# Gate and up projections of a feed-forward layer by seven block products in place of eight, in two passes over the tokens

## Chip, cores and metric

One Trainium2 chip, one core of it. The metric is the device time of one execution in microseconds (us), median over runs. The granted clock of TensorE is given as a share of full speed.

## What is computed

One step of a one-layer encoder over 1024 prompt tokens and 32 sample tokens (1056 in all, width 1024): input projection, two kinds of attention, output projection with residual, and a feed-forward part. The change lies in the last:

```python
def residual_tail(h, oa, ob, g_out_a, g_out_b, w_out, g_ffn, w_gate, w_up, w_down):
    mixed = jnp.concatenate([rmsnorm(oa, g_out_a), rmsnorm(ob, g_out_b)], axis=-1)
    h = h + mixed @ w_out
    u = rmsnorm(h, g_ffn)
    return h + (jax.nn.silu(u @ w_gate) * (u @ w_up)) @ w_down
# then rmsnorm(h, g_final); everything float32; w_gate, w_up: 1024 x 2816, w_down: 2816 x 1024
```

## The kernel before

A matrix product in float32 is made of three TensorE products of type fp32r: each operand x is split into a rounded half `hi` (made on ACT by a copy that rounds) and the rest `lo` = x - `hi` (made on DVE), and `product` (L603 to L606) adds hi·hi, hi·lo and lo·hi in one PSUM bank. In `product`'s lines L604 is the first, L605 the second, L606 the third. PSUM has eight banks of 512 float32 columns.

Five programs run side by side, one for each engine (`@block.tensor` for PE, `scalar` for ACT, `vector` for DVE, `gpsimd` for POOL, `sync` for SP, which issues the loads and stores), each strictly in the order written, tied by semaphores (`wait_ge`, `then_inc`).

The stage before the feed-forward part (`out_product`, `turn_mixed`, `turn_residual`) makes h by tiles of 128 tokens. `turn_residual` (L984) turns each tile twice on PE, by eight 128x128 transposes each: h itself (L987 to L990, into banks 4 and 5, kept as the columns to which the result is added, `outs`) and the normalised u (banks 6 and 7), which ACT and DVE split into `f_hi` and `f_lo`.

The feed-forward part takes the 2816 hidden columns in eleven pairs of 128-column blocks (`FFQ`), tokens along the free dimension in three chunks of 384, 384 and 288 (`CHUNKS`). For each pair q, `gate_up(q)` (L1009) makes gate and up of both blocks: four weights of 1024x128 by eight k-blocks by three chunks. Silu is ACT's (L1459), the product gate·up DVE's (L1877), and h is split by ACT (L1465) and DVE (L1880). Then `down(q - 1)` (L1030) multiplies the hidden pair before with the down weights, 24 groups (eight output blocks by three chunks) of six matmuls, in banks 6 and 7 by turns, and DVE adds each group to `outs` (`add_one`, L1883). Each weight is loaded once (`ffn_load`, L2324, three raw buffers of 512 KB), and split by ACT (L1092) and DVE (L1522, 128x1024). POOL has nothing to do in this part. The last pair's groups use four banks, 4 to 7 (`last_down`), and between them and behind them `turn_out` turns the result back to rows, which ACT squares and DVE scales (`last_out`).

## Time and profile before

| | |
|---|---|
| runs | 1424.62, 1425.41, 1426.76 us (median 1425.41) |
| profiled execution: span | 1425.3 us |
| PE busy | 1389.4 us (97%), 9041 matmuls |
| DVE, ACT, POOL busy | 572.3, 484.7, 213.8 us |
| stage before the feed-forward part | 567 to 635 us of the span |
| feed-forward part | from 635.1 us to the end |
| moved by DMA | 97.64 MB, mean 69 GB/s |

The profile comes from one execution; the page gives no other time of it than the span, from its first to its last instruction. Busy times are shares of an engine's own time. A matmul's duration in it covers its whole way through the array, and the next one starts long before it ends, so the rate is read from starts.

### The profile page before, as it was taken

What the parts mean: (1) busy time and instruction counts of PE and PEld (TensorE: products, weight loads), DVE (VectorE), ACT (ScalarE), POOL (GpSimd) and SP (SyncE); (2) the same over time, 40 slices, a digit from 0 to 9 for tenths busy, and PEclk for the clock granted to TensorE, in tenths of its full rate; (3) what the DMA queues carried; (4) which work ended last, traced back from release to release, by engine and by line L of the source; (5) the groups of instructions that cost most, each with busy time, mean ns of one, the idle gap of its engine ahead of it and who ended that gap; (6) DMA issues with size and microseconds to landing.
All of it is one profiled execution on the core that took longest, in us unless ns stands there. A gap on an engine that the chain in (4) does not pass through costs nothing.

```text
span 1425.3 us, 22561 instructions
## 1 busy us (share of the span) xinstructions
PE 1389.4 (97%) x9041; PEld 1288.1 (90%) x9041; DVE 572.3 (40%) x1340; ACT 484.7 (34%) x1049; POOL 213.8 (15%) x318
## 2 busy tenths in 40 slices
PE   7999999999999899999999999999999999999998
PEld 5988898788878677889999999999999999999997
DVE  6345634242323433562333434342424252525156
ACT  6356555655554552563212121212121212121103
POOL 3145551644443230000000000000000000000000
PEclk9999999999999899999999999999999999999999
DMA  7621124212120444314202020202020202020003
GB/s 202 115 67 38 32 78 156 81 43 80 51 83 15 150 163 135 109 46 132 61 30 68 22 74 16 74 16 74 16 74 16 75 16 74 16 74 15 30 1 122
DMA packets 110255, 97.64 MB, mean 69 GB/s; under 512 B 15936, under 2 KB 96928, under 8 KB 109640
## 3 DMA queue, kind: packets, MB, share of 16 engines
q1 hardware_dynamic: 110152, 96.20, 23.0%
q8 instruction: 72, 1.18, 0.4%
q14 instruction: 31, 0.25, 0.1%
HBM read 77.07 MB, written 19.21 MB: 68 GB/s over the span
## 4 chain that ended last, share of the span: by engine, by line
PE 91%; DVE 3%; DMA 2%; ACT 2%; issue 2%; POOL 1%; SPq 0%; ACTq 0%; DVEq 0%
PE ps L604 28%; PE ps L605 26%; PE ps L606 26%; PE ps L808 2%; DMA cb<-c_scratch 1%; PE ps L738 1%; PE ps L956 1%; PE ps L820 1%; PE ps L685 1%; PE ps L897 1%; PE ps L776 1%; DVE ps L1650 1%; DMA ob<-o_scratch 1%; ACT sp_x L1279 0%; PE ps L703 0%
## 5 line engine op out<-in xcount | busy, mean ns | idle before, releaser
L1891 DVE TENSOR_TENSOR outs<-outs,ps 128x384 f32<-128x384 f32 (+1 forms) x264 | 134.5, 509 | 108.3 <-PE ps L606 108.0
L1877 DVE TENSOR_TENSOR gu<-ps,sg 128x384 f32<-128x384 f32 (+1 forms) x66 | 34.6, 524 | 237.8 <-PE ps L606 237.8
L2055 POOL TENSOR_TENSOR pl_x<-sp_x,ph_x 128x512 fp32r<-128x512 f32 (+5 forms) x120 | 102.3, 866 | 170.4 <-ACT sp_x L1279 169.0
L1465 ACT ACTIVATE h_hi<-gu 128x384 fp32r<-128x384 f32 (+1 forms) x66 | 32.9, 498 | 222.4 <-DVE gu L1877 222.4
L1278 ACT ACTIVATE ph_x<-ps,negc 128x512 fp32r<-128x512 f32 (+5 forms) x120 | 63.0, 525 | 84.5 <-PE ps L820 84.5
L1459 ACT ACTIVATE sg<-ps 128x384 f32<-128x384 f32 (+1 forms) x66 | 30.5, 465 | 171.7 <-PE ps L606 171.7
L604 PE MATMUL ps<-f_hi,ff0hi 128*128 128x384 f32 (+1 forms) x264 | 85.7, 325 | 0.0
L604 PE MATMUL ps<-f_hi,ff2hi 128*128 128x384 f32 (+1 forms) x264 | 85.6, 324 | 0.0
L604 PE MATMUL ps<-f_hi,ff3hi 128*128 128x384 f32 (+1 forms) x264 | 85.6, 324 | 0.0
L604 PE MATMUL ps<-f_hi,ff1hi 128*128 128x384 f32 (+1 forms) x264 | 85.6, 324 | 0.0
L605 PE MATMUL ps<-f_lo,ff0hi 128*128 128x384 f32 (+1 forms) x264 | 85.3, 323 | 0.0
L605 PE MATMUL ps<-f_lo,ff1hi 128*128 128x384 f32 (+1 forms) x264 | 85.2, 323 | 0.0
L605 PE MATMUL ps<-f_lo,ff2hi 128*128 128x384 f32 (+1 forms) x264 | 85.2, 323 | 0.0
L605 PE MATMUL ps<-f_lo,ff3hi 128*128 128x384 f32 (+1 forms) x264 | 85.2, 323 | 0.0
L606 PE MATMUL ps<-f_hi,ff0lo 128*128 128x384 f32 (+1 forms) x264 | 85.2, 323 | 0.0
L606 PE MATMUL ps<-f_hi,ff1lo 128*128 128x384 f32 (+1 forms) x264 | 85.1, 322 | 0.0
L606 PE MATMUL ps<-f_hi,ff2lo 128*128 128x384 f32 (+1 forms) x264 | 85.1, 322 | 0.0
L606 PE MATMUL ps<-f_hi,ff3lo 128*128 128x384 f32 (+1 forms) x264 | 85.1, 322 | 0.0
L604 PE MATMUL ps<-h_hi,ff4hi 128*128 128x384 f32 (+1 forms) x240 | 82.2, 342 | 0.6 <-DVE outs L1894 0.5
L604 PE MATMUL ps<-h_hi,ff5hi 128*128 128x384 f32 (+1 forms) x240 | 78.2, 326 | 0.0
L1092 ACT ACTIVATE ff4hi<-raw 128x1024 fp32r<-128x1024 f32 x10 | 10.6, 1060 | 197.0 <-PE ps L606 197.0
L605 PE MATMUL ps<-h_lo,ff5hi 128*128 128x384 f32 (+1 forms) x240 | 77.5, 323 | 0.0
(303 smaller groups left out, 3837.5 us busy)
## 6 DMA issues: line engine op xcount, KB each, us to landing
raw<-in_w_gate SPq DMA_DIRECT2D x22, 512.0 KB, 4.5
raw<-in_w_up SPq DMA_DIRECT2D x22, 512.0 KB, 5.0
raw<-in_w_down SPq DMA_DIRECT2D x22, 512.0 KB, 3.9
raw<-in_w_in SPq DMA_DIRECT2D x14, 512.0 KB, 4.0
cb<-c_scratch SPq DMA_DIRECT2D x4, 1312.0 KB, 7.1
xt<-in_x_prompt SPq DMA_DIRECT2D x8, 512.0 KB, 4.7
out<-outb SPq DMA_DIRECT2D x16, 256.0 KB, 2.8
ob<-o_scratch SPq DMA_DIRECT2D x16, 256.0 KB, 3.1
```

Source lines behind the costliest of these rows:

```text
L604: pe.matmul(out, wh, xh, start=start, stop=False)
L605: pe.matmul(out, wh, xl, start=False, stop=False)
L606: return pe.matmul(out, wl, xh, start=False, stop=stop)
L685: mm = pe.transpose(ps[0:m, b, (2 * kv + x) * P:(2 * kv + x + 1) * P], ot_w[kv][:, x * m:(x + 1) * m], ident[:])
L738: pe.matmul(ps[0:rows, 2 + kv, 0:2 * m].rearrange("p (x q) -> p x q", x=2), keys[hs, k0:k0 + rows], queries[half][hs, :, q], start=(part = ...
L808: pe.matmul(ps[0:rows, b + h, 0:n], keys[i % 2][hs, k0:k0 + rows], queries[i % 2][hs, q], start=(part == 0), stop=False)
L1278: act.activation(ph_x[2 * (v % 2) + h][0:rows, 0:n], ps[0:rows, b + h, 0:n], ACT.Exp, bias=decay, scale=-1.0)
L1459: act.activation(sg[c][:, 0:n], bank(c, n), ACT.Silu).then_inc(S["g_sg"], 1)
L1465: act.activation(h_hi[par][:, f, c0:c0 + n], gu[(f + c) % 2][:, 0:n], ACT.Copy).then_inc(S["g_hi"], 1)
L1877: dve.tensor_tensor(gu[(f + c) % 2][:, 0:n], bank(3 + c, n), sg[c][:, 0:n], ALU.mult)\
L1891: add = dve.tensor_tensor(y, y, bank(b, whole * P).rearrange("p (t m) -> p t m", t=whole), ALU.add)
L2055: pool.tensor_tensor(pl_x[at][0:rows, 0:n], sp_x[at][0:rows, 0:n], ph_x[at][0:rows, 0:n].bitcast(F32), ALU.subtract).then_inc(S["x_pl"], 1)
```

## The change

Gate and up of one 128-column block are the two block rows of a 2x2 matrix A: row 1 is gate, row 2 is up, column 1 the upper 512 rows of the weights, column 2 the lower. The input u (1024 x tokens) is cut in the same way: k halves by token halves. The 2x2 product of blocks is then made by seven products and 15 additions instead of eight products. The changed kernel

- runs over the tokens in two passes, 512 tokens in halves of 256 and 544 in halves of 272 (`HALF_OF`), with 22 sets in each (`SETS` = 44, one set for each block of 128 hidden columns), so all gate, up and down weights are loaded and split twice;
- makes per set seven products (`ffn_product`), each of four k-blocks and one token half, in banks 0 to 5 by turns; ACT copies two of the seven banks out (`copy_out`), DVE adds the other five (`add_bank`), POOL adds two more parts (`add_fourth`), then silu and gating are done in SBUF (`silu`, `gated`);
- makes four sums of weight blocks per set on POOL (`weight_sums`, from raw weights in `fraw`, 1 MB in two buffers), and four sums of input blocks per pass (`input_sum`); ACT and DVE split seven weight blocks of 128x512 per set into eleven slots (`SLOTS`), and seven input blocks per pass;
- makes down groups (`down_group`) in the midst of the products, one output half (four output blocks) of a hidden pair per set: four groups of 512 columns in pass 0, eight of 272 in pass 1, always in banks 6 and 7; the down weights' `lo` halves are made by POOL (`down_lo`, 128x1024) from the single buffer `draw`;
- no longer turns h on PE: h goes to DRAM (`x2_dram`) by rows, comes back at the end (`hrow`), and the turned result is added to it by rows (`add_row`); rows 0 to 3 are turned in set 24, added there and scaled in set 25.

The core of the diff:

```diff
-            def turn_residual(t):
-                pe.wait_ge(S["c_h2"], 2 * (t + 1))
-                if t >= 1:
-                    pe.wait_ge(S["d_y"], 4 * t)
-                rows_to_columns(t, xc[t % 2], (4, 5), S["c_t2"])
...
+            def ffn_product(g, i):
+                p = pass_of(g)
+                n, e = HALF_OF[p], 7 * g + i
+                pe.wait_ge(S["fw_lo"], e + 1)
+                if g % NF == 0:
+                    pe.wait_ge(S["u_lo"], 7 * p + U_ORDER.index(i) + 1)
+                if e >= SPARE:
+                    pe.wait_ge(*bank_read(*divmod(e - SPARE, 7)))
...
+                w, (uh, ul) = fw[e % SLOTS], fu[i]
+                for k in range(4):
+                    mm = product(bank(e % SPARE, n), w[:, 0, k, :], w[:, 1, k, :], uh[:, k, 0:n], ul[:, k, 0:n],
+                                 k == 0, k == 3)
+                mm.then_inc(S["f_pe"], 1)
...
+            def down_group(n, q, j):
...
+                pe.wait_ge(S["f_hl"], 4 * pg + 4)
+                pe.wait_ge(S["dw_lo"], n - 1)
+                if at >= 2:
+                    pe.wait_ge(S["y_add"], at - 1)
...
+            for g in range(SETS):
+                for i in range(7):
+                    ffn_product(g, i)
...
+                    elif g >= 2 and 2 <= i < 6:
+                        down_piece(g, i - 2)
...
+            def weight_sums(g):
...
+                pool.wait_ge(S[f"fw_in{g % 2}"], 32 * (g // 2 + 1))
+                if g >= 1:
+                    pool.wait_ge(S["fw_lo"], 7 * (g - 1) + 5)
+                pool.tensor_tensor(s1, a21, a22, ALU.add).then_inc(S["fw_sum"], 1)
+                pool.wait_ge(S["fw_sum"], 4 * g + 1)
+                pool.tensor_tensor(s2, s1, a11, ALU.subtract).then_inc(S["fw_sum"], 1)
+                pool.tensor_tensor(s3, a11, a21, ALU.subtract).then_inc(S["fw_sum"], 1)
+                pool.wait_ge(S["fw_sum"], 4 * g + 2)
+                if g >= 1:
+                    pool.wait_ge(S["fw_lo"], 7 * (g - 1) + 6)
+                pool.tensor_tensor(s4, a12, s2, ALU.subtract).then_inc(S["fw_sum"], 1)
...
+            def add_fourth(g):
+                n, par = HALF_OF[pass_of(g)], g % 2
+                for x in range(2):
+                    pool.wait_ge(S["f_x"], 2 * g + 2)
+                    pool.wait_ge(S["f_add"], 5 * g + 3 + x)
+                    part = x23[par][:, x, 0:n]
+                    pool.tensor_tensor(part, part, p7[:, 0:n], ALU.add).then_inc(S["f_p7"], 1)
+            def down_lo(n):
...
+                pool.wait_ge(S["dw_hi"], n - 1)
+                pool.tensor_tensor(dw[n % 2][:, 1, :, :], draw[:], dw[n % 2][:, 0, :, :].bitcast(F32), ALU.subtract)\
+                   .then_inc(S["dw_lo"], 1)
...
+            for g in range(SETS):
...
+                if g + 2 < SETS:
+                    weight_sums(g + 2)
+                add_fourth(g)
+                down_lo(g + 1)
...
+            def load_ffn_raw(g):
...
+                elif g >= 2:
+                    sp_.wait_ge(S["fw_lo"], 7 * (g - 2) + 7)
+                    sp_.wait_ge(S["fw_sum"], 4 * (g - 2) + 4)
+                for mat, src in enumerate((w_gate_v, w_up_v)):
+                    sp_.dma_start(fraw[g % 2][:, mat, :, :], src[:, :, f * P:(f + 1) * P]).then_inc(S[f"fw_in{g % 2}"], 16)
+            def load_down_raw(n):
...
+                if n > 2:
+                    sp_.wait_ge(S["dw_lo"], n - 2)
...
+            for k in range(SETS):
+                load_ffn_raw(k + 2)
+                if k >= 1:
+                    load_down_raw(k + 2)
```

**Order on SP.** The loads of two steps of the feed-forward part, before:

```order
L2106 DMA raw_61<-in_w_down 128x1024 [waits cw_lo]
L2106 DMA raw_62<-in_w_down 128x1024 [waits cw_lo]
L2106 DMA raw_60<-in_w_gate 128x8x128 [waits cw_lo]
L2106 DMA raw_61<-in_w_up 128x8x128 [waits cw_lo]
L2106 DMA raw_62<-in_w_gate 128x8x128 [waits cw_lo]
L2106 DMA raw_60<-in_w_up 128x8x128 [waits cw_lo]
```

and now, two sets in pass 0 (`fraw` the raw gate and up weights, `draw` the raw down weights):

```order
L2635 DMA draw<-in_w_down 128x2x512 [waits dw_lo]
L2626 DMA fraw_175<-in_w_gate 128x8x128 [waits fw_sum,fw_lo]
L2626 DMA fraw_175<-in_w_up 128x8x128
L2635 DMA draw<-in_w_down 128x2x512 [waits dw_lo]
L2626 DMA fraw_176<-in_w_gate 128x8x128 [waits fw_sum,fw_lo]
L2626 DMA fraw_176<-in_w_up 128x8x128
```

Before, every load waited for the split of the same kind of weight (`cw_lo`, counted on DVE); now each pair of gate and up loads stands behind a down load that waits for POOL's `down_lo` (`dw_lo`).

**Order on POOL.** POOL had no row in the feed-forward part; its last ones were the attention's. Now one set in pass 0 has (`sums` the weight sums, `x` and `p` the parts that `add_fourth` adds, `dw` the split down weights):

```order
L2330 TENSOR_TENSOR sums<-fraw_176 128x512 [waits fw_lo,fw_in0]
L2332 TENSOR_TENSOR sums<-sums,fraw_176 128x512 [waits fw_sum]
L2333 TENSOR_TENSOR sums<-fraw_176 128x512
L2337 TENSOR_TENSOR sums<-fraw_176,sums 128x512 [waits fw_lo,fw_sum]
L2363 TENSOR_TENSOR x_0_190<-x_0_190,p_179 128x256 [waits f_add,f_x] x2
L2370 TENSOR_TENSOR dw_218<-draw,dw_218 128x1024 [waits dw_hi]
```

Four sums, two adds and one down half repeat in every set, all from SBUF to SBUF.

**Order on DVE.** Before, between two pairs (`ff` the split weights, `gu` the product of gate and up):

```order
L1522 TENSOR_TENSOR ff0lo<-raw_60,ff0hi 128x1024 [waits cw_hi]
L1522 TENSOR_TENSOR ff1lo<-raw_61,ff1hi 128x1024 [waits cw_hi]
L1522 TENSOR_TENSOR ff2lo<-raw_62,ff2hi 128x1024 [waits cw_hi]
L1877 TENSOR_TENSOR gu_191<-ps,sg_187 128x384 [waits g_lo,g_sg,g_mm]
L1880 TENSOR_TENSOR h_lo_186<-gu_191,h_hi_185 128x384 [waits g_hi]
L1877 TENSOR_TENSOR gu_190<-ps,sg_188 128x384 [waits g_lo,g_sg,g_mm]
L1880 TENSOR_TENSOR h_lo_186<-gu_190,h_hi_185 128x384 [waits g_hi]
L1877 TENSOR_TENSOR gu_191<-ps,sg_189 128x288 [waits g_lo,g_sg,g_mm]
L1880 TENSOR_TENSOR h_lo_186<-gu_191,h_hi_185 128x288 [waits g_hi]
```

and now, from the last weight half of a set in pass 0 to the second bank add of the next (`fw` the split weights, `sg` the gate part, `x` the up part, `y` the result):

```order
L2007 TENSOR_TENSOR fw_192<-sums,fw_192 128x512 [waits fw_hi]
L2043 TENSOR_TENSOR sg_220<-sg_220,x_0_190 128x256 [waits f_p7,f_sg]
L2065 TENSOR_TENSOR y<-y,ps 128x512 [waits y_add,d_pe]
L2050 TENSOR_TENSOR h_lo_215<-sg_220,h_hi_214 128x256 [waits f_hh]
L2033 TENSOR_TENSOR x_0_190<-x_0_190,ps 128x256 [waits f_p7,f_pe]
L2043 TENSOR_TENSOR sg_220<-sg_220,x_0_190 128x256 [waits f_add,f_sg]
L2007 TENSOR_TENSOR fw_193<-sums,fw_193 128x512 [waits fw_hi]
L2007 TENSOR_TENSOR fw_194<-sums,fw_194 128x512 [waits fw_hi]
L2050 TENSOR_TENSOR h_lo_215<-sg_220,h_hi_214 128x256 [waits f_hh]
L2033 TENSOR_TENSOR sg_216<-x_199,ps 128x256 [waits f_x,f_pe]
L2007 TENSOR_TENSOR fw_195<-sums,fw_195 128x512 [waits fw_hi]
L2033 TENSOR_TENSOR x_1_222<-x_199,ps 128x256 [waits f_x,f_pe]
```

The gating now reads only SBUF and waits for POOL (`f_p7`), and the add to `y`, the hidden half and the bank adds of the next products stand behind it.

## Rows read from the trace of the kernel before

**Rows 1.** The page: busy time by engine (share of span), and the clock granted to PE in 40 slices.

```profile
span 1425.3 us, 22561 instructions
PE 1389.4 (97%) x9041; PEld 1288.1 (90%) x9041; DVE 572.3 (40%) x1340; ACT 484.7 (34%) x1049; POOL 213.8 (15%) x318
...
PEclk9999999999999899999999999999999999999999
```

**Rows 2.** Busy times of each engine, granted clock, DMA share and GB/s, in three stretches.

```profile
567.00:635.10 68.10, 67.78 (x376) 55.74 (x376) 41.80 (x72) 37.97 (x86) 0.00 (x0) 1.00 0.27 83
...
705.00:775.00 70.00, 70.00 (x433) 69.59 (x432) 26.05 (x50) 11.59 (x18) 0.00 (x0) 1.00 0.16 46
...
1370.00:1388.00 18.00, 16.66 (x103) 15.70 (x102) 11.09 (x27) 0.00 (x0) 0.00 (x0) 1.00 0.00 1
```

**Rows 3.** Timeline of PE in one gate and up weight: start us, us, form.

```profile
999.74 0.34 PE L604 MATMUL ps<-f_hi,ff3hi 128*128 128x384 f32 x1
...
1007.11 0.29 PE L604 MATMUL ps<-f_hi,ff3hi 128*128 128x288 f32 x1
...
1010.30 0.34 PE L604 MATMUL ps<-h_hi,ff4hi 128*128 128x384 f32 x1
```

**Rows 4.** Timeline of PE: six matmuls of 256 columns in a row.

```profile
100.10 0.28 PE L604 MATMUL ps<-ph_w,vs_hi 128*128 128x256 f32 x1
...
100.69 0.28 PE L606 MATMUL ps<-ph_w,vs_lo 128*128 128x256 f32 x1
```

**Rows 5.** Timeline of PE: matmuls of 512 columns, then turned tiles (x8).

```profile
621.95 0.40 PE L604 MATMUL ps<-wo_hi,m_hi 128*128 128x512 f32 x1
...
626.15 1.03 PE L956 MATMUL ps<-ident,xb 128*128 128x128 f32 x8
627.02 1.04 PE L956 MATMUL ps<-ident,raw 128*128 128x128 f32 x8
```

**Rows 6.** Groups by form, DVE: xcount, busy us, mean ns, idle before.

```profile
L1583 DVE TENSOR_TENSOR vw_lo<-cache_v,vw_hi 128x256 fp32r<-128x256 f32 x4 | 1.7, 423 | 3.0 <-ACT vw_hi L1225 3.0
L1585 DVE TENSOR_TENSOR vw_lo<-outb,vw_hi 128x512 fp32r<-128x512 f32 x8 | 5.6, 702 | 13.8 <-ACT vw_hi L1225 13.8
```

**Rows 7.** Groups by form, ACT and POOL.

```profile
L1360 ACT ACTIVATE ob<-ob 128x512 f32<-128x512 f32 x8 | 5.0, 626 | 4.5 <-DMA ob<-o_scratch 4.5
...
L1247 ACT ACTIVATE ph_w<-sp_w 128x256 fp32r<-128x256 f32 x60 | 24.6, 409 | 29.0 <-DVE sp_w L1662 29.0
...
L2055 POOL TENSOR_TENSOR pl_x<-sp_x,ph_x 128x512 fp32r<-128x512 f32 x48 | 60.8, 1287 | 61.2 <-ACT sp_x L1279 61.2
L2004 POOL TENSOR_TENSOR pl_w<-sp_w,ph_w 128x256 fp32r<-128x256 f32 x60 | 43.0, 738 | 41.4 <-ACT sp_w L1248 41.3
...
L1989 POOL TENSOR_TENSOR cw1lo<-raw,cw1hi 128x1024 fp32r<-128x1024 f32 x9 | 21.8, 2425 | 40.1 <-ACT cw1hi L1092 39.8 <-issue 0.2
```

**Rows 8.** Timelines of POOL and of DVE: two-SBUF-input DVE instructions beside POOL.

```profile
17.80 2.41 POOL L1989 TENSOR_TENSOR cw0lo<-raw,cw0hi 128x1024 fp32r<-128x1024 f32 x1 [9.47 <-ACT cw0hi L1092]
29.68 2.41 POOL L1989 TENSOR_TENSOR cw1lo<-raw,cw1hi 128x1024 fp32r<-128x1024 f32 x1 [9.47 <-ACT cw1hi L1092]
...
17.23 1.28 DVE L1528 TENSOR_TENSOR u_lo<-ps,u_hi 128x512 fp32r<-128x512 f32 x2
...
19.31 1.98 DVE L1734 SCALAR_TENSOR_TENSOR xn<-xt,small,gains 128x1024 f32<-128x1024 f32 x1
...
31.20 1.98 DVE L1734 SCALAR_TENSOR_TENSOR xn<-xt,small,gains 128x1024 f32<-128x1024 f32 x1
```

**Rows 9.** SP's queue: three loads issued in a row, and their landing (DMA view, 649 to 659).

```profile
650.05 0.37 SPq L2106 DMA_DIRECT2D raw<-in_w_gate  x1
...
651.09 1.32 SPq L2106 DMA_DIRECT2D raw<-in_w_gate  x1
...
raw<-in_w_gate SPq DMA_DIRECT2D x2, 512.0 KB, 5.4
```

**Rows 10.** The stretch 460 to 480: PE's busy time and clock (columns as in Rows 2).

```profile
460.00:480.00 20.00, 14.70 (x107) 10.85 (x108) 11.00 (x25) 13.39 (x27) 5.16 (x6) 0.74 0.46 147
```

811 lines of the change are left out of this document (511 added, 300 removed).

## The prediction, made before the change was run

> **What bounds the kernel now.** I read the page first: PE is busy for 97% of the span at an almost undisturbed clock, DVE for 40%, and POOL's 213.8 us all lie before the feed-forward part [rows 1, 2]. Then the windows: in a step of two blocks (705 to 775) PE has no idle time, DVE works 26 us, ACT 12 us, POOL nothing [rows 2]. So the feed-forward part lasts as long as its matmuls stream, and what counts is start to start, not the duration of one (they overlap).
>
> Start to start: 42 matmuls of 384 columns in 7.37 us are 0.1755 us each, 24 of 288 columns in 3.19 us are 0.1329 [rows 3]; 256 columns take 0.118 (five intervals in 0.59) [rows 4]; 512 take 0.2333 (18 intervals in 4.20) [rows 5]. For 272 I take 0.1255, between 256 and 288.
>
> Check on before: gate and up are 2112 matmuls of 384 and 1056 of 288, 511.0 us; down 1056 and 528, 255.5 us; together 766.5.
>
> **The change on PE.** Seven products of four row blocks replace eight: per set 84 matmuls, so 22 x 84 of 256 (218.1 us) and 22 x 84 of 272 (231.9), together 450.0 against 511.0: **-61 us**. Down keeps its columns: 528 of 512 and 1056 of 272, 255.7, no change. A set with down then needs 15.5 us in pass 0 (84 x 0.118 + 24 x 0.2333) and 16.6 in pass 1 (132 x 0.1255). The residual's eight turns per tile go; eight take 0.87 us [rows 5], nine tiles at most 7.3. That stage is PE's (67.8 busy of 68.1) but ACT has 38 us there [rows 2] and now gets seven input splits: I count **-6**, between 0 and -7.3. Near 1370 to 1388 PE stands 1.3 us [rows 2], tied to the old last weights: -1. The turned output tiles stay. If nothing else waits: 1425 - 68 = **1357**.
>
> The Trainium skill (TensorE: Matmul & The Clock Gate, Back-to-back issue gap) gives N/2.4 + 2.5 ns from matmul to matmul. By that estimate gate and up would fall from 473 to 416 us, a gain of 57; the rows are about 8% slower than it, and the sum goes by the rows.
>
> **The change beside PE, and why cover may end.** In sets 2 to 43 each engine's order repeats. Per set DVE has seven weight halves of 128x512, four adds of results (eight narrower ones in pass 1), five bank adds, two gatings and two hidden halves. An instruction of 512 columns takes 0.70 us, one of 256 takes 0.42 [rows 6]; behind another it adds 0.60 (1.28 for two, less 0.68 for one [rows 8]) and 0.34 (the same 0.08 less). That is 6.6 + 3.1 = 9.7 us. ACT: 0.63 and 0.41 each [rows 7], seven weights, one 1024 wide, six narrow ones, about 8 us. POOL, new here: four sums of 1.27, two adds of 0.74, one down half of 2.42 [rows 7], 9.0 us. Each alone fits into 15.5, hidden by PE's matmuls. Three things chain them.
>
> (1) *A ring through SP's queue.* The load of the down weights waits until POOL has made the last down half (single buffer), and SP's gate and up loads for the set after next stand behind it in the queue; POOL's next sums need these. Three loads issued in a row at 650.05 have landed at 651.09 + 5.4 = 656.5 [rows 9], 6.4 us; with two semaphore hops 6.6. Ring: 6.6 + 5.1 + 1.5 + 2.4 + 0.3 for waits on POOL's own results = **15.9 us**, against PE's 15.5: +0.4 in pass 0, nothing in pass 1.
>
> (2) *DVE and POOL hold each other up.* At 19.31 a DVE instruction with both inputs in SBUF takes 1.98 us: POOL's instruction began at 17.80 and ended at 20.21, and DVE ended 1.08 later. The same at 31.20 (POOL 29.68 to 32.09), 1.98 again, while DVE's pair at 17.23, one input in PSUM, kept its 1.28 beside POOL [rows 8]. So such a DVE instruction waits out POOL's, and ends some 0.2 earlier than its duration behind it. The weight halves (`weight_lo_ffn`), gatings (`gated`) and hidden halves (`hidden_lo`), 11 of DVE's 20 instructions and 6.6 us if each stood alone, are of this kind; before, POOL was idle here. No row shows POOL held by DVE. I take it to work both ways, since DVE was held to the very end of POOL's instruction, as by something that one of them has to itself; one way alone is a bound below. The Trainium skill (SBUF — State Buffer, Who interferes with whom) has a rule against this change: the two engines take turns at a shared pair of ports, and whoever comes second waits for the whole instruction of the first. By that rule, the trace agrees for DVE (1.98 against 1.28).
>
> (3) *The gating sits behind POOL's adds.* DVE's `gated(g, 1)` waits for POOL's second add of `add_fourth(g)`, after which POOL starts `down_lo` at once and holds DVE for another 2.2 us; queued behind it on DVE are the y add that frees a down bank, the hidden half and the bank adds, for which PE and ACT wait.
>
> By hand, from the end E of a down half: DVE's held weight half 0.5, gating, y add, hidden half, bank add, gating: +2.5; ACT's hidden, bank copy and two weights 2.0: +4.5; two weight halves (the first overlaps) and the hidden half: +5.6, where the first down group of an even set may start; bank add, ACT's silu and weight: +6.9. The loads land at +6.6 and POOL's sums begin. From here sums and weight halves alternate: sum to 7.9, half 8.4, sum 9.6, bank add, y add and half 10.1, sum 11.3, half 11.8, sum 13.0, bank add and half 13.5, POOL's first add 14.1, y and bank adds 14.5, second add 15.2, down half: **E' = 17.6**. Without the lock it is 15.9. So in pass 0 a set takes 17.6 instead of 15.5: 20 sets, **+42** (with one direction 16.6: +22; unlocked +8). In pass 1 the narrow adds lengthen it to about 18.0 against 16.6; 20 sets, **+29** (bounds 0 and +45).
>
> Smaller terms: the first sets run from loads issued within set 0, so set 2's first down group waits about 5 us for sums, hidden and down halves: **+5** (0 to 10). Where the passes meet, four POOL sums of 2.4 and seven DVE halves of 1.2 (128x1024, twice the 512 form) come into the ring: **+12** (5 to 20). Rows 0 to 3 are added and scaled in sets 24 and 25, eight DVE instructions of about 1.2, half of them of the locked kind: **+5**. The last 16 groups alternate between two banks where 24 had four, then rows are squared, rooted and scaled: **+3** (-3 to 8). DMA moves twice the gate and up weights, about 1.5 MB a set; the share before is 0.16 [rows 2], so bandwidth costs nothing, only the latency above does.
>
> Sum: 1357 + 42 + 29 + 5 + 12 + 5 + 3 = **1453 us**. It is made against the profiled span, 1425.3, which is the median of the runs shown (1425.41) within 0.1.
>
> **Rivals.**
> *Faster: the lock falls beside the ring.* If DVE mostly meets POOL while it waits for loads, or POOL's instructions are not held, DVE keeps up and the ring of 15.9 is all: 1357 + 8 + 0 + 4 + 10 + 3 + 3 = **1385**. For it: DVE has 5.8 of 15.5 us free, and POOL stands 6.6 us of each ring. Against: DVE has just its serial stretch (E to +6.9) in that pause, and its weight halves come with the sums. It decides for a set time under 16.8 us on the mean of both passes, where the added waits no longer eat the 68.
>
> *Slower still: PE's clock.* In my forecast PE stands about 4 us ahead of the first down group of every second set. At 460 to 480, with 5.3 us idle in the stretch, the clock was 0.74 instead of 1.00 [rows 10]. A fall to the lower level in each of these gaps costs PE some 2 us in a pair of sets, which delays the bank add that POOL waits for: 20 pairs, +40, **1493**. Against: most gaps would be split between several waits. The Trainium skill (TensorE: Matmul & The Clock Gate, Why this matters for your kernels) also warns of idle gaps between bursts of matmuls.
>
> *The seven products save nothing on PE* would need matmuls of 256 columns no faster than 0.135 us; [rows 4] speaks against it, and I give it no chance of its own.
>
> **How the numbers follow.** Forecast 0.50, the lock beside the ring 0.38, the clock 0.12. Forecast's own range: 1422 (one direction only in both passes, small terms low) to 1480. The other cases extend the range to 1380 and 1495; below lies some of the first rival, above some of the last. About 0.2% (2.9 us) is what a measurement of this kernel can tell from no change: 0.04 lies there, the lower edge of the forecast gives 0.01 to faster, so 0.39 faster, 0.57 slower.
>
> **What would show it.** Right: PE's 256-column matmuls 0.118 apart; in pass 0 idle PE ahead of a down group in even sets, ended by DVE's hidden half; set times near 17.6 and 18.0; DVE's weight halves at 0.7 alone and up to 2 us beside POOL; POOL idle some 6.6 us a set until gate and up weights land; SP waiting for POOL's down half. Wrong: PE without gaps in pass 0, or set times at 15.5 to 16 (then the rival); a granted clock clearly below 1 in the feed-forward part (then the other); or gaps that end with an engine I have not named.

## The result, and the profile after

The changed kernel takes **1566.9 us** (median of 4 runs, 1564.4 to 1572.1), the kernel before 1426.1 beside it: ratio 1.0996, 95% interval [1.0971, 1.102]. It is slower by 10%. The prediction said slower, with 1453 in a range up to 1495: the direction held, the size did not, and the time lies 72 us above the range. The profiled run took 1564.7, its span is 1562.9.

Short names below: a *set* is one block of 128 hidden columns, its time read from the first matmul of product 0 to the next such; a *weight half* is the `hi` (ACT) or `lo` (DVE) part of a 128x512 weight, the *down half* is `down_lo`, the *hidden half* `h_hi` or `h_lo`; *gating* is `gated`, a *bank add* `add_bank`, a *y add* `add_group`. In the changed kernel `product`'s three lines are L702 to L704; line numbers in a view are those of the kernel that it shows, so they shift a little from run to run.

The page of the changed kernel, where [rows 1] stood:

```profile
span 1562.9 us, 26068 instructions
PE 1380.0 (88%) x9497; PEld 1245.5 (80%) x9497; DVE 945.2 (60%) x1760; ACT 674.2 (43%) x1462; POOL 685.3 (44%) x634
...
PEclk9999999999999999989999999987998999999998
```

PE is busy for 1380 us where it was 1389, although gate and up should cost it 61 us less: much of the difference went by at a lower clock. The windows, in four stretches of the feed-forward part (sets 0 to 3, 4 to 19, 20 to 27, and from set 43 to the end); columns as in [rows 2]:

```profile
632.13:708.12 75.99, 58.63 (x395) 54.60 (x394) 57.14 (x77) 34.08 (x69) 42.67 (x30) 0.87 0.28 78
...
708.12:1009.10 300.98, 266.36 (x1731) 244.65 (x1730) 224.53 (x320) 111.64 (x224) 165.03 (x113) 0.93 0.31 85
1009.10:1210.46 201.36, 154.71 (x994) 146.17 (x993) 142.30 (x192) 70.75 (x131) 94.07 (x62) 0.86 0.28 84
...
1506.64:1562.90 56.26, 36.61 (x270) 35.56 (x268) 33.87 (x55) 13.34 (x26) 7.17 (x5) 0.87 0.17 61
```

The first number behind start and end is the length of the stretch. Sets 4 to 19 take 301.0 / 16 = 18.8 us each, where PE needs 15.5. Sets 28 to 42 take 19.75 each (1210.46 to 1506.64), where PE needs 16.6. The eight sets around the pass change take 201.

The matmuls themselves did what [rows 4] said. PE's timeline: from the first to the last of these there are eight intervals of 256 columns in 0.94 us, 0.1175 each.

```profile
817.27 0.28 PE L702 MATMUL ps<-fu5hi,fw 128*128 128x256 f32 x1
...
818.21 0.28 PE L704 MATMUL ps<-fu5hi,fw 128*128 128x256 f32 x1
```

The view of waits (engine, line, releaser: us in total, times, longest):

```profile
POOL sums L2330 <- DMA fraw<-in_w_up: 294.9, 34, 26.4
...
DVE fw L2007 <- ACT fw L1543: 181.3, 171, 5.0
...
PE ps L702 <- DVE h_lo L2050: 91.2, 21, 10.1
...
POOL sums L2330 <- DVE fw L2007: 71.2, 9, 10.6
...
PE ps L702 <- DVE y L2065: 30.6, 18, 4.4
```

PE stands for DVE's hidden half, as forecast, 21 times. POOL's first sum of a set waits mostly for the load, as forecast too. The second row is the one that I had not counted: DVE waits about one microsecond, 171 times, for ACT's half of a weight. At 804.16 below this is the time that ACT takes behind DVE's last bank add for a silu and the half; DVE's own half starts 0.65 us after the start of ACT's.

The instruction groups show the lock (us in all, mean ns of one); the same forms alone take 700 and 420 ns [rows 6], 2420 ns on POOL [rows 7]:

```profile
L2007 DVE TENSOR_TENSOR fw<-sums,fw 128x512 fp32r<-128x512 f32 x176 | 195.0, 1129 | 138.4 <-ACT fw L1543 138.4
...
L2007 DVE TENSOR_TENSOR fw<-fraw,fw 128x512 fp32r<-128x512 f32 x132 | 153.5, 1175 | 42.9 <-ACT fw L1543 42.8
...
L2043 DVE TENSOR_TENSOR sg<-sg,x 128x256 f32<-128x256 f32 (+1 forms) x88 | 68.7, 781 | 8.4 <-POOL x L2363 3.5 <-DVE x L2033 0.5
```

One turn of POOL, in its timeline (start us, us, engine, line, operation; in brackets how long the engine stood before it, and what ended that); beside it DVE's instructions of the same time, then ACT's:

```profile
803.30 0.74 POOL L2363 TENSOR_TENSOR x<-x,p 128x256 f32<-128x256 f32 x1 [1.31 <-DVE sg L2033]
803.99 2.43 POOL L2370 TENSOR_TENSOR dw<-draw,dw 128x1024 fp32r<-128x1024 f32 x1
814.65 1.32 POOL L2330 TENSOR_TENSOR sums<-fraw 128x512 f32<-128x512 f32 x1 [8.22 <-DMA fraw<-in_w_up]
816.04 1.64 POOL L2332 TENSOR_TENSOR sums<-sums,fraw 128x512 f32<-128x512 f32 x1
817.63 1.76 POOL L2333 TENSOR_TENSOR sums<-fraw 128x512 f32<-128x512 f32 x1
819.36 1.75 POOL L2337 TENSOR_TENSOR sums<-fraw,sums 128x512 f32<-128x512 f32 x1
821.08 1.43 POOL L2363 TENSOR_TENSOR x<-x,p 128x256 f32<-128x256 f32 x2
822.46 2.89 POOL L2370 TENSOR_TENSOR dw<-draw,dw 128x1024 fp32r<-128x1024 f32 x1
```

```profile
804.16 2.81 DVE L2007 TENSOR_TENSOR fw<-sums,fw 128x512 fp32r<-128x512 f32 x1 [1.01 <-ACT fw L1543]
806.89 0.41 DVE L2043 TENSOR_TENSOR sg<-sg,x 128x256 f32<-128x256 f32 x1
...
809.02 0.43 DVE L2043 TENSOR_TENSOR sg<-sg,x 128x256 f32<-128x256 f32 x1 [0.46 <-DVE x L2033]
810.73 1.29 DVE L2007 TENSOR_TENSOR fw<-sums,fw 128x512 fp32r<-128x512 f32 x2 [1.28 <-ACT fw L1543]
```

```profile
809.48 0.42 ACT L1592 ACTIVATE h_hi<-sg 128x256 fp32r<-128x256 f32 x1 [1.73 <-DVE sg L2043]
809.81 0.37 ACT L1577 ACTIVATE x<-ps 128x256 f32<-128x256 f32 x1
810.07 1.14 ACT L1543 ACTIVATE fw<-sums 128x512 fp32r<-128x512 f32 x2
```

From the end of one down half (806.42) to that of the next (825.35) are 18.9 us. POOL waits 8.2 for the load, the four sums take 6.4 instead of 5.1 (so DVE holds POOL too: 1.75 against 1.29 alone in [rows 7]), the adds 1.4, the down half 2.9. In all of sets 4 to 19 POOL's turn goes through the load: on the mean 7.6 us of landing, 6.2 of sums, 2.4 of adds with their waits, 2.6 of down half, together 18.8. In every second set the adds take 3.1 to 3.5 us, because one of them waits for DVE's bank add (803.30), and that for PE. On DVE the weight half at 804.16 is held to 806.97, 2.8 us instead of 0.7, with the gating behind it. And ACT stands 1.7 us for DVE's second gating before it comes to two weight halves that depend on no gating at all; DVE then waits 1.3 for these.

PE in the same pair, and its clock (windows; the number before the last two is the granted clock):

```profile
830.38 0.50 PE L702 MATMUL ps<-h_hi,dw 128*128 128x512 f32 x1 [4.16 <-DVE h_lo L2050]
```

```profile
826.20:830.40 4.20, 0.04 (x2) 0.02 (x1) 2.82 (x8) 1.72 (x4) 0.00 (x0) 1.00 0.97 268
830.40:832.40 2.00, 2.00 (x6) 1.62 (x7) 0.99 (x3) 1.46 (x3) 0.00 (x0) 0.64 0.94 225
832.40:834.40 2.00, 2.00 (x11) 1.91 (x10) 1.79 (x3) 0.00 (x0) 1.43 (x2) 0.51 0.03 8
834.40:838.40 4.00, 4.00 (x27) 3.61 (x27) 2.11 (x4) 2.34 (x4) 4.00 (x3) 1.00 0.00 0
```

Behind 4.2 us of standing PE runs 4 us at a mean of 0.575 (the lower level, 1.2 GHz, for most of it) and loses 4 x 0.425 = 1.7 us. So, by this estimate, the gap costs PE 5.9 us, not 4.2.

### The profile page after: what moved, and what is told of

It reads as the page before. It is cut to its first block, busy times and chain, and to the rows that moved or that the text cites. A ratio compares the mean times of both kernels' runs of the same rounds, so it can differ in the third digit from the quotient of the medians.

```text
span 1562.9 us, 26068 instructions
## 1 busy us (share of the span) xinstructions
PE 1380.0 (88%) x9497; PEld 1245.5 (80%) x9497; DVE 945.2 (60%) x1760; ACT 674.2 (43%) x1462; POOL 685.3 (44%) x634
## 4 chain that ended last, share of the span: by engine, by line
PE 51%; DVE 19%; issue 11%; ACT 6%; DMA 4%; POOL 2%; SPq 1%; DVEq 0%; ACTq 0%; POOLq 0%
PE ps L702 15%; PE ps L703 14%; PE ps L704 14%; DVE fw L2007 5%; ACT fw L1543 3%; DVE sg L2043 3%; PE ps L906 2%; DVE y L2065 2%; DMA fraw<-in_w_up 2%; DVE h_lo L2050 2%; DVE x L2033 2%; DVE sg L2033 1%; PE ps L836 1%; DMA cb<-c_scratch 1%; ACT x L1577 1%
## 5 line engine op out<-in xcount | busy, mean ns | idle before, releaser
L702 PE MATMUL ps<-h_hi,dw 128*128 128x272 f32 (+1 forms) x528 | 186.6, 353 | 125.8 <-DVE h_lo L2050 91.2
L2007 DVE TENSOR_TENSOR fw<-sums,fw 128x512 fp32r<-128x512 f32 x176 | 195.0, 1129 | 138.4 <-ACT fw L1543 138.4
L702 PEld LDWEIGHTS ps<-h_hi,dw 128*128 128x128 f32 x528 | 106.8, 202 | 140.0 <-DVE h_lo L2050 95.6
L704 PE MATMUL ps<-h_hi,dw 128*128 128x272 f32 (+1 forms) x528 | 181.6, 344 | 0.0
L703 PE MATMUL ps<-h_lo,dw 128*128 128x272 f32 (+1 forms) x528 | 181.0, 343 | 0.0
L2007 DVE TENSOR_TENSOR fw<-fraw,fw 128x512 fp32r<-128x512 f32 x132 | 153.5, 1175 | 42.9 <-ACT fw L1543 42.8
L1543 ACT ACTIVATE fw<-fraw 128x512 fp32r<-128x512 f32 x132 | 82.2, 626 | 122.3 <-PE ps L704 102.1
L2065 DVE TENSOR_TENSOR y<-y,ps 128x272 f32<-128x272 f32 (+1 forms) x240 | 117.7, 511 | 18.6 <-PE ps L704 18.6
L704 PEld LDWEIGHTS ps<-h_hi,dw 128*128 128x128 f32 x528 | 107.7, 204 | 8.8
L2370 POOL TENSOR_TENSOR dw<-draw,dw 128x1024 fp32r<-128x1024 f32 x44 | 111.2, 2528 | 5.1 <-ACT dw L1568 5.1
L703 PEld LDWEIGHTS ps<-h_lo,dw 128*128 128x128 f32 x528 | 107.6, 204 | 4.4
L1543 ACT ACTIVATE fw<-sums 128x512 fp32r<-128x512 f32 x176 | 104.4, 619 | 1.1 <-PE ps L704 0.9
L702 PE MATMUL ps<-u_hi,cw1hi 128*128 128x384 f32 (+1 forms) x216 | 75.1, 348 | 1.0 <-POOL cw1lo L2222 1.0
L702 PE MATMUL ps<-u_hi,cw0hi 128*128 128x384 f32 (+1 forms) x216 | 75.0, 347 | 0.0
```

Of the source, the lines that this page charges most:

```text
L702: pe.matmul(out, wh, xh, start=start, stop=False)
L703: pe.matmul(out, wh, xl, start=False, stop=False)
L704: return pe.matmul(out, wl, xh, start=False, stop=stop)
L1543: act.activation(fw[e % SLOTS][:, 0, :, :], weight_block(g, i), ACT.Copy).then_inc(S["fw_hi"], 1)
L2007: dve.tensor_tensor(lo, weight_block(g, i), hi.bitcast(F32), ALU.subtract).then_inc(S["fw_lo"], 1)
L2065: dve.tensor_tensor(dst, dst, bank(6 + at % 2, width), ALU.add).then_inc(S["y_add"], 1)
```

## The experiments

All start from the changed kernel. The times are medians, the ratios (with 95% interval) against the kernel before, run beside them.

**1. The queue.** In SP's loop:

```diff
+            load_ffn_raw(2)
             for k in range(SETS):
-                load_ffn_raw(k + 2)
+                load_ffn_raw(k + 3)
                 if k >= 1:
                     load_down_raw(k + 2)
```

> Only the order on SP's queue changes: gate and up weights of a set are loaded ahead of the down weights that wait for POOL's down half, so that the ring through the queue is open. Theory 1 (ring of load, sums, adds and down half, stretched by the lock between DVE and POOL): POOL stands no longer 6.6 to 8 us a set for the landing; the held work that DVE and POOL must take in turn is 6.6 + 9.0 = 15.6 us a set, so a set falls from 18.8 to 16 to 17 in pass 0 and from 19.75 to 17 to 18 in pass 1: about -45 and -40, and some 10 at the start and where the passes meet, 1460 to 1490. Rival (the serial chain of DVE, ACT and POOL behind product 5 sets the set's time, the loads only fill a pause that is there anyway): POOL's pause stays and ends with DVE in place of the DMA, under 20 us are gained, 1550 or more.

1567.0 us, 1.0993 [1.0967, 1.102]: not a microsecond. POOL's 295 us of waiting for the load shrank to the one wait at the start, and the time stands in other rows:

```profile
POOL sums L2330 <- DVE fw L2007: 244.9, 42, 10.6
...
POOL x L2363 <- DVE x L2033: 118.7, 42, 12.8
...
POOL sums L2330 <- DMA fraw<-in_w_up: 26.2, 1, 26.2
```

So the rival held: another path of the same length lies beside the ring through the queue, and my own theory of one ring falls here. One turn of it in POOL's timeline:

```profile
813.12 1.37 POOL L2330 TENSOR_TENSOR sums<-fraw 128x512 f32<-128x512 f32 x1 [5.74 <-DVE fw L2007]
...
820.92 1.07 POOL L2363 TENSOR_TENSOR x<-x,p 128x256 f32<-128x256 f32 x1 [1.62 <-DVE x L2033]
```

The sums' buffer is single, and POOL may write it only when DVE has made the weight halves from it; that ends its first wait. But with the sums done POOL stands again, in every set, for a bank add of DVE, which waits for PE's product. So the path does not close through the buffer of the sums. It goes from POOL's down half to DVE's held weight half and gating, ACT, DVE's weight halves and hidden half, PE, DVE's bank add and POOL's adds. Sets 4 to 19 took 18.7 us each (18.8 in the change), sets 28 to 42 took 20.4 where they had taken 19.75, and sets 20 to 27 took 5 us less in all. Why pass 1 got longer is open.

**2 and 3. The down half on VectorE**, alone and with the queue's order. `down_lo` moves word for word to DVE:

```diff
                 weights_lo(g, 3)
+                down_lo(g + 1)
```

> Only the down weights' second halves move, from GpSimd to VectorE behind the seventh weight half of a set. Theory 1: the ring loses 2.4 us and the hold of the gating by the down half; DVE has 1.2 us more of 15.5, which it can carry. The ring is still there through POOL's sums and adds, but the load of the down weights now waits for an instruction of VectorE in the middle of the set: set times 16 to 17 in pass 0, about 17 to 18 in pass 1, 1460 to 1490. Rival (VectorE is the engine that is late in every chain): 1.2 us more on it a set make each set 0.5 to 1.2 longer, 1590 to 1620.

> Both edits at once. Theory 1: POOL has 6.6 us a set and waits for no load; what DVE and POOL take in turn is 7.8 + 6.6 = 14.4 us, under PE's 15.5, so sets come near PE's own 15.5 to 16 and 16.6 to 17.2: 20 x 3 and 20 x 2.8 from the change's 1567, and 15 to 25 at the start and the pass change: 1415 to 1435. If the two edits open one and the same ring, both together give hardly more than the better of the two (within 15 us of it). Rival (VectorE late in every chain): no better than the change.

Alone 1495.6, 1.0489 [1.0458, 1.0521], both 1497.5, 1.0505 [1.0489, 1.0521]. Giving the engine that seemed late 1.2 us more work a set gained 71 us: 2.4 us are gone from POOL's part of both rings, and with them the hold of DVE's last weight half or gating (2.81 and 2.66 us in the timeline of the change). The order of the queue again gave nothing. Number 2 lies 6 us above its 1460 to 1490, far from the rival's 1590; for both together the 1415 to 1435 was wrong, and what came is the case set beside it, hardly more than the better of the two edits. In pass 1 each set took 18.3 us, with DVE waiting 1.3 for ACT's first two weight halves in each. Number 2 takes away two things at once, the hold in front of the gating and 2.4 us of POOL's work; its 71 us are for both.

**4. No sums of weights** (products 2 to 5 take raw weights; POOL's `weight_sums` and the waits for it are gone):

```diff
-            if i in SUM_OF:
-                return sums[:, SUM_OF[i], :, :]
-            mat, k = (A11, A12)[i] if i < 2 else A22
+            mat, k = (A11, A12, A11, A12, (1, 0), A22, A22)[i]
```

> Leaves out the four sums of weights that POOL makes in each set (products 2 to 5 take raw weights in their place; the same loads, halves, matmuls and adds are made). POOL keeps two adds and the down half, 3.9 us a set. Theory 1: neither ring nor alternation of sums and weight halves is left, DVE's held time is at most 3.9 a set: sets at 15.5 to 16.2 and 16.6 to 17.3; the input sums where the passes meet stay, with 10 us of it: 1400 to 1425. Rival (the chain behind product 5 alone, with the down half on POOL behind the adds): the gap ahead of the first down group stays at over 3 us in pass 0, sets at 17.5 or more, over 1480. The price of the clock rival is in this run too: without gaps of 4 us, the granted clock of the stretch should be over 0.98 where the change had 0.946 in all.

1527.3, 1.0707 [1.0689, 1.0725]. With 5.1 us a set taken from POOL there remain sets of 17.1 in pass 0 and 20.2 in pass 1, and the down half still holds DVE for 2.8 us ahead of the gating. So 5.1 us of POOL's work a set were worth 40 us, and 2.4 us at that place 71. The 1400 to 1425 was wrong. The time lies where the rival had it (over 1480), but pass 0 is shorter than its 17.5, and the gap is 2.3 us and not over 3.

Pass 1 shows the second path bare, and longer than the 19.75 of the change:

```profile
1303.86 0.77 POOL L2341 TENSOR_TENSOR x<-x,p 128x272 f32<-128x272 f32 x1 [14.28 <-DVE x L2028]
```

```profile
1307.76 2.83 DVE L2002 TENSOR_TENSOR fw<-fraw,fw 128x512 fp32r<-128x512 f32 x1 [1.02 <-ACT fw L1538]
```

```profile
1318.73 0.36 PE L700 MATMUL ps<-h_hi,dw 128*128 128x272 f32 x1 [1.89 <-DVE y L2060]
```

POOL stands 14.3 us for a bank add, so neither sums nor loads make this set 20 us long. What does is DVE's held half (2.83 us beside the down half), ACT and DVE behind it, and a y add for which PE waits before it may go on.

The clock: in sets 4 to 19 PE stands 2.3 to 2.5 us in each of eight sets. Behind three of these gaps the granted clock was 0.50 or 0.51 in the next two us, the lower level, and the set took 19.4 to 19.6 us; behind the other five it was 1.00, and the set took 18.0 to 18.2. One of each:

```profile
808.34 0.50 PE L700 MATMUL ps<-h_hi,dw 128*128 128x512 f32 x1 [2.35 <-DVE h_lo L2045]
```

```profile
841.83 0.80 PE L700 MATMUL ps<-h_hi,dw 128*128 128x512 f32 x1 [2.34 <-DVE h_lo L2045]
```

**5 and 6. ScalarE's order**, alone and with the queue's. The first two weight halves go ahead of the hidden half:

```diff
             for g in range(SETS + 1):
+                if g < SETS:
+                    weights_hi(g, 0)
                 if g >= 1:
                     hidden_hi(g - 1, 0)
...
-                weights_hi(g, 0)
                 silu(g, 0)
```

> ScalarE takes the two weight halves at the start of a set ahead of the hidden half and the bank copy, nothing else changes. Theory of two rings of nearly one length (one by SP's queue and the landing, one by VectorE: down half on GpSimd, held weight half and gating, hidden half and weight halves on ScalarE, weight halves on VectorE, the sums' buffer free, sums, adds, down half): this shortens the second ring alone, by 1.3 us or more, and the first stays; within 12 us of the change's 1567. Rival (PE's gap ahead of the first down group, which ends with VectorE's hidden half, is itself what costs): the hidden half comes 1.3 us sooner in every second set, 25 to 30 us gained, 1540.

> The same order on ScalarE and in addition the order on SP's queue of e1_queue. Two rings: now both are shorter, a set falls by 1.3 to 1.5 us from 18.8 and 19.75: 1505 to 1520, although neither edit alone gains more than 12 us. Rival (gap alone): the same as ScalarE's order alone gives, since the queue gave nothing.

Alone 1520.4, 1.0669 [1.0653, 1.0685], with the queue 1491.6, 1.046 [1.0443, 1.0477]. Both came out lower than expected: the 12 us allowed for the first and the 1505 of the second were wrong. The order of ACT alone gained 47. Before and after it POOL's turn goes through the load; what fell in sets 4 to 19 is the adds with their waits (2.4 to 1.7 us), since PE and DVE's bank adds came sooner, and the hold of the down half (2.6 to 2.4). So the two paths are not apart: POOL's sums, adds and down half lie on both, and in every second set of the change the second one reached into the first. With it shortened the ring through the load shows nearly bare. POOL's first sums of two sets in the kernel with ACT's order alone:

```profile
804.63 1.32 POOL L2331 TENSOR_TENSOR sums<-fraw 128x512 f32<-128x512 f32 x1 [7.62 <-DMA fraw<-in_w_up]
...
822.46 1.31 POOL L2331 TENSOR_TENSOR sums<-fraw 128x512 f32<-128x512 f32 x1 [7.62 <-DMA fraw<-in_w_up]
```

17.8 us, all of them through the load. Now the queue's order, worth nothing before, gains 29: 12 in sets 4 to 19 (now 17.1 each), 15 in sets 20 to 27, and only 1 in sets 28 to 42 (18.5 to 18.4). In pass 0 that is what two paths in parallel do: each hides what the other is worth. In pass 1 the path through PE goes on to bind: with both edits POOL still stands in each set for DVE's bank adds (1.8 and 2.3 us at 1300), and PE for a hidden half or a y add.

**7. Nothing on GpSimd in the sets** (sums, fourth adds and down half on DVE, SP's order). On DVE:

```diff
                 weights_lo(g, 1)
+                sums_dve(g + 2, 0)
                 add_bank(g, 2)
...
                 weights_lo(g, 2)
+                sums_dve(g + 2, 1)
...
                 add_bank(g, 4)
+                sums_dve(g + 2, 2)
...
                 weights_lo(g, 3)
...
+                down_lo(g + 1)
+                fourth(g, 0)
...
                 add_bank(g, 5)
+                sums_dve(g + 2, 3)
                 weights_lo(g, 4)
+                fourth(g, 1)
```

> From set 2 on GpSimd makes nothing in the sets: sums, fourth adds and down half stand on VectorE, with SP's order of e1_queue (GpSimd keeps the eight input sums and the sums of sets 0 and 1). Nobody holds VectorE: its weight halves should last 0.69 in a stretch in the middle of a pass where they lasted 0.98 and 1.16 on the mean in e3_both. Against e3_both VectorE has 3.1 us more work a set and loses 2.7 us of holds. If VectorE's string of work and of waits for ScalarE sets the time, about the same as e3_both, 1485 to 1515. If the holds themselves were what is late, sets at 15.5 to 16.5: 1420 to 1450.

1506.6, 1.057 [1.0553, 1.0588], inside the 1485 to 1515 expected if DVE's own string of work sets the time. The weight halves between 700 and 960 with POOL idle; in the kernel with both edits (3) they lasted 944 and 1103 ns there:

```profile
L2007 DVE TENSOR_TENSOR fw<-sums,fw 128x512 fp32r<-128x512 f32 x57 | 38.2, 690 | 38.0 <-ACT fw L1543 38.0
...
L2007 DVE TENSOR_TENSOR fw<-fraw,fw 128x512 fp32r<-128x512 f32 x45 | 30.1, 684 | 7.8 <-ACT fw L1543 7.8
```

The holds are gone and the time is no better: what DVE gains it works off itself.

**8. Three edits**: SP's order, the down half on DVE, ACT's order.

> ScalarE's order, SP's order and the down half on VectorE, that is e3_both with ScalarE's order. In e3_both VectorE waits 1.30 us of each set for ScalarE's first two weight halves, behind the hidden half; that wait goes, a set of pass 1 falls from 18.28 to about 17.0 and a pair of pass 0 by 2 to 2.5: 1497 - 20 x 1.3 - 20 x 1.1 = 1450. If another wait on ScalarE takes its place, half of it: 1475.

1441.8, 1.0118 [1.0103, 1.0133]. ACT's order is worth 56 on top of (3). Sets of 16.0 and 17.4.

**9. A wait in front of the down half**: in POOL's loop

```diff
                 add_fourth(g)
+                pool.wait_ge(S["f_gu"], 2 * g + 1)
                 down_lo(g + 1)
```

> The change with one wait more: GpSimd starts the down half of a set only when VectorE has done the gating `gated(g, 1)`. Nothing is moved to another engine and GpSimd's own string gets about 1 us longer. Theory of the second ring with the held gating: the last weight half and the gating pass unheld, the hidden half of ScalarE comes about 1.5 to 2 us sooner relative to the fourth adds; the down half and what follows it on the queue of loads come about 1 us later. By the ring through the loads alone this is a loss of about 1 us a set (1600); by the ring through VectorE a gain; together (the longer one counts) between 1550 and 1600. Rival (only total work held matters, not where): no change within 10 us.

1561.8, 1.0957 [1.0938, 1.0975]. A wait more and 5 us less, inside both the range and the rival's "within 10": this one does not tell them apart. With the down half behind the gating, and still on POOL, nearly nothing is won; but POOL's turn still goes through the load in sets 4 to 19, and its down half with the new wait now takes 3.4 us of it instead of 2.6. So the edit made one path longer (pass 0: 18.8 to 19.2 us a set) and perhaps the other shorter (pass 1: 19.75 to 19.1), and how the 71 us of number 2 divide between the place and the work stays open.

**10. VectorE's order**: in the kernel with three edits the second bank add goes ahead of the weight half, the down half behind the third piece (set 24 keeps the old order of the first two).

```diff
                 add_bank(g, 1)
...
-                weights_lo(g, 1)
                 add_bank(g, 2)
+                weights_lo(g, 1)
...
                 weights_lo(g, 3)
-                down_lo(g + 1)
...
                 add_piece(g, 2)
+                down_lo(g + 1)
```

> e8_three with two moves in VectorE's order: the second bank add ahead of the weight half for which it waited on ScalarE, and the down half behind the third piece of down adds. In e8_three's second pass PE waits about 0.5 to 0.6 us twice in a set for y adds that stand behind these two: a set of 17.4 should fall to 16.6 to 17.0, in pass 0 a pair by up to 1: 1420 to 1435. If VectorE's holds merely move to the next instruction: 1442 as before.

1425.2, 0.9995 [0.9986, 1.0004]: the time of the kernel before. Two sets of pass 0, four of pass 1, and the eight at the pass change:

```profile
796.38:827.40 31.02, 31.02 (x219) 28.87 (x217) 27.49 (x43) 14.07 (x28) 15.84 (x12) 1.00 0.36 102
1203.00:1270.00 67.00, 67.00 (x529) 66.47 (x528) 58.34 (x100) 28.39 (x56) 30.73 (x24) 1.00 0.34 95
...
951.53:1118.80 167.27, 142.53 (x995) 135.15 (x993) 138.01 (x203) 71.39 (x131) 74.30 (x52) 0.94 0.34 104
```

PE has no gap left in these stretches; sets take 15.5 and 16.8 us. What is left of the loss lies at the start (sets 0 to 3 take 72.1 us, 76.0 in the change), where the passes meet (167, with some 135 of PE's own: two sets of 15.5, six of 16.6, 4 of turned tiles) and at the end (52.3, was 56.3).

**11 and 12. Input sums of the second pass**: behind the weight sums of their set, and left out (of the kernel with three edits; products 2, 3, 4 and 6 take plain quarters). In POOL's loop:

```diff
-                if g == NF - 2:
-                    input_sum(1, 0)
-                if g == NF - 1:
-                    input_sum(1, 1)
-                    input_sum(1, 2)
                 if g == NF:
                     input_sum(1, 3)
                 if g + 2 < SETS:
                     weight_sums(g + 2)
+                if g == NF - 2:
+                    input_sum(1, 0)
+                if g == NF - 1:
+                    input_sum(1, 1)
+                    input_sum(1, 2)
```

> e9_order with GpSimd's first three input sums of the second pass behind the weight sums of their set, where they were ahead of them (in e8_three GpSimd stood 6.1 us for VectorE at 983.9 ahead of such a sum, with the weight sums behind it until 991). Theory: the sets 20 to 24 have 10 to 15 us less, the rest is the same: 1408 to 1425. Rival: the wait of PE at 1014 (9.0 us, for the hidden half) is due to VectorE's and ScalarE's input halves, and these come later now: no gain.

> e8_three without the four input sums of the second pass (its products 2, 3, 4 and 6 take quarters of the input as they are; input halves, loads and products stay). This prices them: four of 2.5 us on GpSimd with as much of VectorE held, and the waits for them. Sets 20 to 27 take 171.6 us in e8_three, about 35 more than PE needs. If the sums are the cause of most of it, 20 to 25 us less: 1420. If the fourteen input halves on ScalarE and VectorE and the turned rows are, under 10 us less: over 1432.

Later: 1425.2, 0.9994 [0.9985, 1.0003], no gain; set 20 lost 2.2 us, set 22 lost 1.9, set 21 got 4.4 longer. Left out: 1434.9, 7 less than with them. They are a small part of the pass change (over 1432 was expected in that case; the theory of number 11, 10 to 15 us less, was wrong).

**13 to 15. The rest of the pass change.** 13: rows 0 to 3 squared and scaled one to a set (squares in sets 24 to 27, scaling in 28 to 31). 14: in addition the last three input sums on VectorE, each behind its input half. 15: number 10 without the weight sums. The edits of 13 on ScalarE and VectorE, and of 14 on VectorE (SP's stores and loads of these rows are moved to fit, and GpSimd's first input sum goes behind the weight sums):

```diff
-                if g == NF + 2:
-                    for t in range(4):
-                        out_squares(t)
+                if NF + 2 <= g < NF + 6:
+                    out_squares(g - NF - 2)
...
-                if g == NF + 3:
-                    out_roots(0, 4)
-                    for t in range(4):
-                        out_row(t)
...
+                if g == NF + 6:
+                    out_roots(0, 4)
+                if NF + 6 <= g < NF + 10:
+                    out_row(g - NF - 6)
                 add_bank(g, 4)
```

```diff
                     input_lo(1, 0)
+                    input_sum_dve(1)
...
                     input_lo(1, 1)
+                    input_sum_dve(2)
...
                     input_lo(1, 3)
+                    input_sum_dve(3)
```

> e9_order with the squares (ScalarE) and the scaling (VectorE) of rows 0 to 3 spread, one row to a set, where they stood four in a row at the end of sets 24 and 25. In e9_order set 26 takes 22.8 us, with PE standing 3.5 us for a hidden half and then some 3.4 us at the lower clock, and set 25 takes 18.5. Theory: the four scalings in a row, 1.2 us each and more when held, delay the next gating; spread, set 26 falls to 17 to 18 and set 25 to 17: 5 to 8 us less, 1417 to 1420. Rival: VectorE has no room for 1.2 us more in a set of 16.8, each spread row costs a set 1 us: 1421 to 1425.

> e13_rows with the last three input sums of the second pass on VectorE, each behind the input half it waits for, and the first on GpSimd behind the weight sums. VectorE gets three instructions of about 1.25 us and loses three holds of up to 2.5. If the sets 20 to 23 (17.8, 22.3, 27.7, 16.1 in e9_order) are long by GpSimd's sums and their holds, 5 to 10 us less than e13_rows. If they are long by VectorE's own amount of work in these sets (seven input halves beside the usual), no change within 3 us or somewhat slower.

> e9_order without GpSimd's four sums of weights in each set (as in e4_no_sums; products 2 to 5 take raw weights). With PE already the bound in the middle of both passes, sets there stay at 15.5 and 16.6 to 16.8. What the sums and their holds cost in e9_order is then only at the start, where the passes meet and at the end: if the holds make these stretches long, 15 to 25 us less (1400 to 1410); if VectorE's own work and its order do, under 8 us less.

13: 1420.8, 0.9963 [0.9949, 0.9976]; sets 20 to 27 from 167.3 to 159.5, and the sets behind them 0.2 longer each, so both the theory and its rival had a part. 14: **1417.9, 0.9945 [0.9933, 0.9958]**, 0.5% faster than the kernel before; sets 20 to 27 in 156.4. The step from 13 is 3 us, which its rival allowed: GpSimd's input sums and their holds are not what makes those sets long. 15: 1405.9, 0.9867 [0.985, 0.9884], 19 us less than number 10: the weight sums with their holds make the stretches long. 10 of them lie in sets 0 to 3 (62.4 against 72.1), 6 in sets 20 to 27. (The edit takes out the holds and the waits for the sums together; in set 1 of number 10, where 8 of the 10 us lie, ACT waits only 0.2 us for a sum, while single weight halves of DVE last up to 1.8 us.) Of number 14 the page, then sets 4 to 19 (with the last microsecond of set 3) and 20 to 27:

```profile
PE 1332.8 (94%) x9497; PEld 1205.8 (85%) x9497; DVE 931.6 (66%) x1807; ACT 676.6 (48%) x1462; POOL 575.7 (41%) x587
```

```profile
703.00:952.04 249.04, 249.04 (x1741) 231.99 (x1739) 220.51 (x337) 113.64 (x226) 126.86 (x97) 1.00 0.37 102
952.04:1108.48 156.44, 138.53 (x994) 132.08 (x993) 131.26 (x199) 66.92 (x125) 68.04 (x49) 0.96 0.32 96
```

Sixteen sets without an idle microsecond on PE, beside 1567 for the change as it stood: the same products, the same loads, 149 us apart by the order of work on three engines and in one queue, and by moving two small kinds of work, the down halves and three input sums, from GpSimd to VectorE.

## Why the prediction was right, and where it was wrong

The miss is 1567 - 1453 = 114 us. By its own terms:

- **PE's saving, right.** Sets of 15.5 and 16.8 us (forecast 15.5 and 16.6) wherever little else binds, and 15.5 and 16.6 without the weight sums (15). The floor of 1357 was reached by no kernel here; the nearest with all work in it is 61 above.
- **The residual's turns, -6: about -3.** The feed-forward part starts at 632.1 against 635.1. The stretch 567 to 632 has gaps for DVE now, up to 2.8 us. The same start lies between 628.9 and 635.1 in the profiles of the experiments, which change nothing ahead of it but the weight sums in two of them, so one profile does not tell -3 from -6.
- **The lock, right**, in both directions, and the end some 0.2 early. The bound "one way only" is out: 1.75 us for POOL's sums against 1.29.
- **Pass 0, 17.6 a set: 18.8, +19 us over 16 sets. Pass 1, 18.0: 19.75, +26 us over 15 sets.** The step that failed is the hand timeline from E, twice. *The landing, 6.6 us, was misread.* I took 5.4, the median of the two gate loads in [rows 9], for the third load. The view of that line alone (`--source L2106`, 649 to 652) gives the three landings:

```profile
DMA to landing us min/median/max: 4.1/5.5/6.6
```

The first took 4.1, the third 6.6: it landed at 657.7, 7.6 us behind the first issue and not 6.4. In the change POOL waits 7.6 us on the mean of sets 4 to 19. With 1.0 us more the hand timeline gives 18.6, so this term alone is 16 of the 19 us of pass 0; sums, adds and down half, with holds, came out at 11.2 against 11.0. *The path beside it was left out.* I let ACT's two weight halves follow "2.0 us" behind the gating as if their place were given by the work; their place is given by ACT's program order, behind a hidden half that waits for DVE, and DVE waits for them again, with PE, the bank adds and POOL's adds behind it. I had most of its pieces and took the ring through the load as the only one, and left out what each hop costs DVE: about 1 us of standing, 171 times. Number 1 shows that a right landing would not have been enough: with the load off the path a set still takes 18.7 us. Numbers 1, 4, 5 and 6 show the path; number 4 shows it at 20.2 us in pass 1 with neither sums nor a wait for a load in it. How the 26 us of pass 1 divide between the two was not measured. The 17.8 us of number 6 beside the forecast's 17.6 is luck: the landing 1.0 larger, sums and adds 0.7 smaller.
- **The clock** was a rival with 0.12, priced at 2 us for a pair. It came true in pass 0, on top of the forecast and not in its place: 1.7 us a gap, granted clock 0.93 in sets 4 to 19 against 1.00 in number 14. All eight gaps of 4.1 to 4.2 us there brought the lower level with them. Its price lies within the lengths above and is not a further term; I should have put it into the sum.
- **First sets, +5; pass change, +12, and rows 0 to 3, +5: the worst of it, 53 of the 114 us, and the second step that failed.** Sets 0 to 3 took 76.0 where my terms give 60 (two of 9.9, two of 17.6, and 5): +16. Sets 20 to 27 took 201 where they give 164 (35 and 108, 4 of turned tiles, and 17 for the terms): +37. I had priced the added instructions one by one, but DVE had no room. Beside 13 to 14 us of work and holds in a set of 15.5 there is space for neither seven input halves of 1.2 us nor four sums of 2.5 that hold it, so they go to the path in full (that is my reading; the prices follow), and through gaps of up to 10 us each with its slow clock. 12 prices the four sums at 7 us, 13 the four rows in a row at 4 to 5, 14 the place of the sums at 3, 15 the weight sums with their holds at 6 there and 10 at the start. The rest, some 20 us at the pass change in number 14, I put down to VectorE's own work there; that is argued, not shown.
- **The end, +3: some +13 more**, what remains of the 114. In every kernel here it is 51 to 57 us from set 43's start; PE stands there for the last hidden half (5 us in number 10) and runs on at the lower clock. The order of the last sixteen groups was not tried.
- **The rival "lock beside the ring", 1385**, asked for DVE and POOL to keep up. With the orders set right and the down halves on DVE they do, in the middle of each pass; the ends kept it from that number.

The Trainium skill (SBUF — State Buffer, Who interferes with whom) states that the two engines take turns, and by it the second to come waits whichever it is; the measured holds of both agree with it (2.81 us on DVE against 0.69, 1.75 on POOL against 1.29). What a hold costs depends on what stands behind the held instruction: number 2 took one such hold away, together with 2.4 us of POOL's work, and gained half of the 141 us, while number 7 took all of them away, for 3.1 us more work on DVE a set, and was no better than number 3.
